# Values of all heads multiplied first as token rows, input with features on partitions

## The chip, the cores and the metric

The kernel runs on one core of one Trainium2 chip. The time is what the device takes for one execution, in microseconds (us). The core has a matrix engine (TensorE, PE in the profile), a vector engine (VectorE, DVE), a scalar engine (ScalarE, ACT), a general engine (GpSimd, POOL) and a queue engine (SyncE, SP) that issues transfers. SBUF is the memory of 128 partitions from which the engines read; PSUM holds the results of PE in 8 banks of 128 x 512 floats.

## What is computed

An encoder layer over two sequences, 512 and 1024 tokens of 1024 features, processed as 1536 token rows. The part that matters here is the mixer:

```python
def hybrid_mixer(h, w_in, w_fnet, lb_f, lb_b, out_norm, w_out):
    proj = h @ w_in                       # h = rms_norm(x, norm_mix)
    u, q, zf, zb, iv, g = jnp.split(proj, cuts, axis=-1)
    ...                                   # u: Fourier mixing, 4 groups of 128
    qh = jax.nn.silu(q)                   # 4 heads of 128
    vh = iv.reshape(bsz, seq, HGRN_HEADS, HGRN_DV)
    k_f, logf_f = hgrn2_gates(zf, lb_f)
    k_b, logf_b = hgrn2_gates(zb, lb_b)
    o_fwd = chunked_gated_recurrence(qh, k_f, vh, logf_f)
    o_bwd = ...                           # the same backwards, with k_b, logf_b
    gate = jax.nn.silu(g)
    y_rec = rms_norm(o_fwd + o_bwd, out_norm) * gate
    return jnp.concatenate([y_fourier, y_rec], axis=-1) @ w_out
```

rms_norm(x) is x * rsqrt(mean(x * x) + eps) * w, per token. Behind the mixer come a router and 16 experts, each of which takes its best tokens.

## The kernel before

A product of 32-bit numbers is made of three matmuls of numbers split in a high and a low part (`three_products`, L62 to L66). `heads_phase` (L255) is the first stage; the transform, the router and the experts follow in code of their own.

**The start.** `InputNorm` (L153) loads the 12 input tiles of 128 token rows, takes the sum of squares with ACT (L195), scales rows on DVE (L224), turns each tile on PE with 8 transposes (L249), copies the high part on ACT (L213) and subtracts the low part on DVE (L237). The features of the normalized input (`big_hi`, `big_lo`) then lie on partitions. From the fourth tile on, PE's turns are interleaved with products V, G and Q of the first block (`EARLY`). `HeadWeights` (L69) loads the projection weights in halves of 128x512 (L88), rounds them on ACT (L92) and subtracts on POOL (L96).

**Projections.** 4 heads x 3 blocks of 512 tokens give NN = 12 rounds n. A head has five: values V, gate G, queries Q and the two forget gates ZF and ZB; 12 more belong to the Fourier groups. Each takes 24 matmuls of 512 columns in two halves, `begin` and `proj`, into one of two banks (`PJ`). V comes out with features on partitions, and event `vt` turns it into token rows (L827, copied by ACT at L578 into `v_tok`).

**Rounds.** A list `timeline` gives one order for all engines. Round n has 8 slots. Slot s holds `level` s: 32 small matmuls (L853) that need ACT's copy of keys (L526), which in turn needs DVE's scaling of keys and queries (L720, L722). Then follow the recurrence steps (`update` on DVE, `inter` on PE), the DVE gates of a projection that ended one slot before (`take_gates`), and halves of coming projections, `FILL` of them: 1, 1, 1, 1, 1, 2, 2, 1. Rounds with n % 3 = 0 carry the recurrence of blocks 1 and 2, those with n % 3 = 1 that of block 0; they end with `square`, `ss` (sum of squares, root on ACT at L626), `rstd`, `bc` (a broadcast by PE, L905) and `out` (the product on DVE, L768). Behind slot 7 come `intra` (L864) and `kt`, the turn of the keys (L872). `out` frees the bank into which `kt` goes. The gates of ZB are the longest on DVE: L695, L697, L699, L700, L701. The last matmuls of the stage are L912. The order itself:

## Time and profile before

| | us |
|---|---|
| median of three executions | 2577.06 |
| lowest and highest | 2575.56, 2579.19 |
| the profiled execution | 2577.25 |
| its span, first to last instruction | 2575.5 |
| PE busy in it | 2520.0 |
| DVE busy, ACT busy | 1649.2, 1366.9 |
| heads stage, from the start to the end of L912 | 568.4 |

The span has three stretches: the heads stage, the transform and router up to about 800 us, and the experts. Round 0 begins (its level 0) at 66.47 us. A row of a timeline gives start and duration in us, the engine, line, operation and its tiles; in brackets the idle time before it and what ended it. A row of `--lines` kind gives a group: busy time, mean ns of one, idle time.

### The profile page before, as it was taken

What the parts mean: (1) busy time and instruction counts of PE and PEld (TensorE: products, weight loads), DVE (VectorE), ACT (ScalarE), POOL (GpSimd) and SP (SyncE); (2) the same over time, 40 slices, a digit from 0 to 9 for tenths busy, and PEclk for the clock granted to TensorE, in tenths of its full rate; (3) what the DMA queues carried; (4) which work ended last, traced back from release to release, by engine and by line L of the source; (5) the groups of instructions that cost most, each with busy time, mean ns of one, the idle gap of its engine ahead of it and who ended that gap; (6) DMA issues with size and microseconds to landing.
All of it is one profiled execution on the core that took longest, in us unless ns stands there. A gap on an engine that the chain in (4) does not pass through costs nothing.

```text
span 2575.5 us, 45337 instructions
## 1 busy us (share of the span) xinstructions
PE 2520.0 (98%) x18610; PEld 2278.5 (88%) x18610; DVE 1649.2 (64%) x1927; ACT 1366.9 (53%) x1559; POOL 266.7 (10%) x238
## 2 busy tenths in 40 slices
PE   8999999999987999999999999999999999999998
PEld 6777777787876999999999999999999999999997
DVE  6555555435387666767666676666767666676667
ACT  6434353424445555555556555555555556555556
POOL 3102020101101010010101101010010101101010
PEclk9999999999997999999999999999999999999999
DMA  4101010135327676676767667676676767667677
GB/s 158 31 17 55 2 55 2 61 122 209 138 96 298 229 253 234 247 252 228 252 228 252 240 241 252 228 252 233 247 252 228 252 228 252 240 241 252 228 253 282
DMA packets 62486, 503.73 MB, mean 196 GB/s; under 512 B 7568, under 2 KB 8080, under 8 KB 37808
## 3 DMA queue, kind: packets, MB, share of 16 engines
q1 hardware_dynamic: 46224, 448.88, 48.0%
q0 software_dynamic: 16160, 53.38, 7.0%
q8 instruction: 77, 1.26, 0.2%
q14 instruction: 25, 0.20, 0.0%
HBM read 465.07 MB, written 37.22 MB: 195 GB/s over the span
## 4 chain that ended last, share of the span: by engine, by line
PE 67%; DVE 1%; ACT 1%; DMA 0%; issue 0%; POOL 0%; POOLq 0%; DVEq 0%; ACTq 0%
PE up_banks_b L2025 15%; PE up_banks_a L2025 15%; PE up_banks_b L2028 6%; PE up_banks_a L2028 6%; PE up_banks_b L2061 2%; PE up_banks_b L2060 2%; PE up_banks_b L2059 2%; PE up_banks_b L2058 2%; PE up_banks_a L2062 2%; PE up_banks_b L2062 2%; PE up_banks_a L2059 2%; PE up_banks_a L2061 2%; PE up_banks_a L2058 2%; PE up_banks_a L2060 2%; PE up_banks_b L2023 1%; PE up_banks_a L2023 1%
## 5 line engine op out<-in xcount | busy, mean ns | idle before, releaser
L1842 DVE TENSOR_TENSOR big_lo<-ew_raw,big_hi 128x4096 fp32r<-128x4096 f32 x192 | 849.6, 4425 | 419.0 <-ACT big_hi L1653 418.9
L1653 ACT CAST big_hi<-ew_raw 128x4096 fp32r<-128x4096 f32 x192 | 697.3, 3632 | 506.5 <-PE up_banks_a L2025 223.7
L2025 PE MATMUL up_banks_b<-x_parts,big_hi 128*128 128x384 f32 x2048 | 582.9, 356 | 0.0
L2025 PE MATMUL up_banks_a<-x_parts,big_hi 128*128 128x384 f32 x2016 | 573.8, 356 | 0.0
L2028 PE MATMUL up_banks_b<-x_parts,big_lo 128*128 128x192 f32 x1792 | 449.0, 251 | 0.0
L2028 PE MATMUL up_banks_a<-x_parts,big_lo 128*128 128x192 f32 x1764 | 442.0, 251 | 0.0
L2025 PEld LDWEIGHTS up_banks_b<-x_parts,big_hi 128*128 128x128 f32 x2048 | 371.0, 189 | 0.0
L2025 PEld LDWEIGHTS up_banks_a<-x_parts,big_hi 128*128 128x128 f32 x2016 | 365.1, 189 | 0.6
L2028 PEld LDWEIGHTS up_banks_b<-x_parts,big_lo 128*128 128x128 f32 x1792 | 341.4, 191 | 0.0
L2028 PEld LDWEIGHTS up_banks_a<-x_parts,big_lo 128*128 128x128 f32 x1764 | 336.1, 191 | 0.6
L64 PE MATMUL bank<-big_hi,w_hi 128*128 128x512 f32 x576 | 236.8, 411 | 0.0
L66 PE MATMUL bank<-big_hi,w_lo 128*128 128x512 f32 x576 | 225.6, 392 | 0.0
L65 PE MATMUL bank<-big_lo,w_hi 128*128 128x512 f32 x576 | 225.3, 391 | 0.0
L1639 POOL DMA_INDIRECT residual<-table,this_token x15 | 24.2, 1613 | 1426.5 <-DVE yp L1956 1426.5
L720 DVE TENSOR_TENSOR kq<-kq,decay 128x512 f32<-128x512 f32 x84 | 58.0, 691 | 175.5 <-PE bank L853 175.5
L66 PEld LDWEIGHTS bank<-big_hi,w_lo 128*128 128x128 f32 x576 | 108.4, 188 | 24.1
L64 PEld LDWEIGHTS bank<-big_hi,w_hi 128*128 128x128 f32 x576 | 108.5, 188 | 22.5
L65 PEld LDWEIGHTS bank<-big_lo,w_hi 128*128 128x128 f32 x576 | 108.7, 189 | 19.2
L526 ACT COPY keys<-kq 128x512 f32<-128x512 f32 x84 | 55.6, 662 | 113.1 <-DVE kq L722 112.5
L96 POOL TENSOR_TENSOR w_lo<-w_raw,w_hi 128x512 fp32r<-128x512 f32 x48 | 72.1, 1515 | 406.8 <-ACT w_hi L92 406.7
L1674 ACT CAST h_parts<-ups 128x384 fp32r<-128x384 f32 x128 | 65.5, 511 | 78.4 <-DVE ups L1908 78.4
L2062 PE MATMUL up_banks_a<-big_lo,h_parts 128*128 128x512 f32 x256 | 99.6, 389 | 0.0
(320 smaller groups left out, 4076.3 us busy)
## 6 DMA issues: line engine op xcount, KB each, us to landing
ew_raw<-in_expert_weights SPq DMA_DIRECT2D x192, 2048.0 KB, 7.8
w_raw<-in_w_heads SPq DMA_DIRECT2D x48, 256.0 KB, 2.8
x_in<-in_x SPq DMA_DIRECT2D x12, 512.0 KB, 4.4
x_d<-in_x POOLq DMA_DIRECT2D x12, 512.0 KB, 4.1
residual<-x_d POOLq DMA_DIRECT2D x12, 512.0 KB, 2.9
ffn_in<-h_and_xT_d POOLq DMA_DIRECT2D x12, 512.0 KB, 2.9
ew_raw<-residual SPq DMA_DIRECT2D x12, 512.0 KB, 6.7
tab<-in_tables POOLq DMA_DIRECT2D x10, 512.0 KB, 7.6
```

Of the source, the lines that this page charges most:

```text
L64: nc.tensor.matmul(out, w_hi, x_hi, start=start, stop=False, skip_group_check=True)
L65: nc.tensor.matmul(out, w_hi, x_lo, start=False, stop=False, skip_group_check=True)
L66: return nc.tensor.matmul(out, w_lo, x_hi, start=False, stop=stop, skip_group_check=True)
L1653: nc.scalar.copy(w_hi[:, c % RING], raw[:, c % RAW]).then_inc(hi_done, 1)
L1842: nc.vector.tensor_tensor(w_lo[:, c % RING], raw[:, c % RAW], w_hi[:, c % RING].bitcast(F32), ALU.subtract).then_inc(lo_done, 1)
L2025: last = nc.tensor.matmul(out[:, 0:2 * CAP], hi, x[:, k], start=n == 0, stop=n == KT - 1, skip_group_check=True)
L2028: nc.tensor.matmul(out[:, ALL_HI], lo, x[:, k, ALL_HI], start=False, stop=False, skip_group_check=True)
L2058: nc.tensor.matmul(s_bank[i], h[:, t, S_HI], hi, start=a, stop=False)
L2059: nc.tensor.matmul(s_bank[i], h[:, t, H_S_LO], hi, start=False, stop=False)
L2060: nc.tensor.matmul(s_bank[i], h[:, t, S_HI], lo, start=False, stop=b)
L2061: nc.tensor.matmul(p_bank[i], h[:, t, H_P_BOTH], hi, start=a, stop=False)
L2062: last = nc.tensor.matmul(p_bank[i], h[:, t, H_P_BOTH], lo, start=False, stop=b)
```

## The change

The host also hands over the input with features on partitions (`x_cols`) and the norm weights as columns. The 96 turns of the input, the 48 turns of the values and their copies disappear. Instead:

- `InputNorm` keeps x as 8 tiles of 128x512 per block. Squares are made on ACT (L234) and added on DVE (L243) into one accumulator; PE sums them over the partitions with a column of ones (`total`, L251, 4 matmuls of one column per block), ACT takes the root, DVE inverts, PE spreads the result over the partitions (`spread`, L272), and DVE multiplies (L279), ACT copies (L295), DVE subtracts (L299).
- Values are made first, for all four heads at once: a stationary tile of 128 tokens, 512 columns of weights (L947 to L949), 12 token tiles of 24 matmuls. The first four tiles use block 0 before it is normalized (only the norm weight is in it, L284, L289); the rows are scaled by ACT when they leave PSUM (L665). Block 0 is normalized last.
- Values are stored to DRAM (L539) and loaded into `v_tok` by head and block (L552).
- Value weights come in four pieces of 128x1024. DVE subtracts the first two, POOL the others (L100).
- The sums and spreads stand at fixed places in PE's products (`lines`).
- The stream of projections has G, Q, ZF and ZB; `FILL` is one half in every slot; in rounds with n % 3 = 0 the gate of the round after next is projected between Q and ZF.

```diff
 LEVELS = 7
 EPS = 1e-6
-HEAD_SRC = (4, 5, 1, 2, 3)
+HEAD_SRC, VALUE_SRC = (5, 1, 2, 3), 4
 NJ = len(HEAD_SRC)
...
+    PIECES = ((0, 1), (2, 3), (4, 5, 6, 7))
+    LINES = [("sum", 0), ("sum", 1), ("spread", 1), ("sum", 2), ("spread", 2), ("spread", 0)]
+    SCALED = ([("rstd", 0), ("rstd", 1)] + [(1, k) for k in range(KT)] + [("rstd", 2)] +
+              [(b, k) for b in (2, 0) for k in range(KT)])
+    SPLIT = [(b, k) for b in ("raw", 1, 2, 0) for k in range(KT)]
...
+    def add(self, dve, b, k):
+        n = KT * b + k
+        dve.wait_ge(self.squared, n + 2)
+        if k > 1:
+            dve.wait_ge(self.added, self.adds(n - 1))
+        elif b:
+            dve.wait_ge(self.totalled, self.LINES.index(("sum", b - 1)) + 1)
+        self.nc.vector.tensor_tensor(self.added_up, self.squares[0] if k == 1 else self.added_up, self.squares[n % 2], ALU.add)\
+            .then_inc(self.added, 1)
...
+    def total(self, pe, b):
+        pe.wait_ge(self.added, (KT - 1) * (b + 1))
+        if b == 2:
+            pe.wait_ge(self.scaled, self.SCALED.index((1, KT - 1)) + 1)
+        for c in range(CH):
+            last = self.nc.tensor.matmul(self.totals[b][:, c:c + 1], self.added_up[:, c * P:(c + 1) * P], self.ones[:],
+                                         start=c == 0, stop=c == CH - 1, skip_group_check=True)
+        last.then_inc(self.totalled, 1)
+
...
+        VALUE_TILES = [(tuple(range(CH)), bank[0:CH])] + \
+                      [((t, t + 1), pair) for t, pair in ((4, o_acc[1:3]), (6, bank[0:2]), (8, bank[2:4]), (10, o_acc[1:3]))]
+        VALUES_OUT = 16 * TT // 2
+        V_FIRST = [16 * NB * len(ks) for ks in norm.PIECES]
...
-            stream += proj(n, V) + [("begin", n, G), ("vt", n), ("proj", n, G)]
-            stream += [e for j in (Q, ZF, ZB) for e in proj(n, j)]
+            ahead = {1: ((n, G), (n, Q), (n + 1, G), (n, ZF), (n, ZB)), 2: ((n, Q), (n, ZF), (n, ZB))}
+            stream += [e for m, j in ahead.get(n % NB, ((n, G), (n, Q), (n, ZF), (n, ZB))) for e in proj(m, j)]
...
-        FILL, LAST_FILL = (1, 1, 1, 1, 1, 2, 2, 1), (2, 2, 2, 1, 1, 1, 1, 1)
+        FILL, LAST_FILL = (1,) * 8, (2, 2, 2, 1, 1, 1, 1, 1)
...
+                for t in range(TT):
+                    sp.wait_ge(v_evicted, t + 1)
+                    sp.dma_start(v_dram[t * P:(t + 1) * P], sig[:, t % 2]).then_inc(sig_used[t % 2], 16)
+
+                def load_values(n):
+
+                    h, b = n // NB, n % NB
+                    if h == 0:
+                        for i in range(2):
+                            sp.wait_ge(sig_used[i], VALUES_OUT)
+                        norm.parted(sp, 1, KT - 1)
+                    else:
+                        filled(sp, ("u", n - NB, 0))
+                        filled(sp, ("u", n - NB, 1))
+                        sp.wait_ge(intra_done, n - NB + 1)
+                    sp.dma_start(v_tok[:, b], v_dram[b * BLK:(b + 1) * BLK, h * P:(h + 1) * P]
+                                 .rearrange("(c p) v -> p c v", p=P)).then_inc(norm.loaded[b], 16)
+
...
+                def evict_values(tiles):
+
+                    for t in tiles:
+                        act.wait_ge(v_filled, 1 + next(i for i, (ts, _) in enumerate(VALUE_TILES) if t in ts))
+                        if t >= 2:
+                            act.wait_ge(sig_used[t % 2], 16 * (t // 2))
+                        value = next(flat(banks[ts.index(t)][:]) for ts, banks in VALUE_TILES if t in ts)
+                        if t < CH:
+                            norm.inverted(act, 0)
+                            nc.scalar.activation(sig[:, t % 2], value, ACT.Identity, scale=norm.rstd[:, t:t + 1])\
+                                .then_inc(v_evicted, 1)
+                        else:
+                            nc.scalar.copy(sig[:, t % 2], value).then_inc(v_evicted, 1)
+
...
+                act.wait_ge(const_loaded, 64)
+                norm.high_raw(act, 0)
+                norm.high_raw(act, 1)
+                weights.high_values(act, 0)
+                norm.high_raw(act, 2)
+                norm.high_raw(act, 3)
+                weights.high_values(act, 1)
+                squares(0, 0, 1, 2, 3)
+                for k in range(4, KT):
+                    norm.high_raw(act, k)
+                squares(0, 4, 5, 6, 7)
+                weights.high_values(act, 2)
+                weights.high_values(act, 3)
+                squares(1, *range(KT))
+                weights.high(act, 0)
+                weights.high(act, 1)
+                norm.root(act, 0)
+                norm.root(act, 1)
+                for k in range(KT):
+                    norm.high(act, 1, k)
+                evict_values(range(0, 4))
+                squares(2, *range(KT))
+                norm.root(act, 2)
+                evict_values((4, 5))
+                for k in range(KT):
+                    norm.high(act, 2, k)
+                evict_values((6, 7))
+                for k in range(KT):
+                    norm.high(act, 0, k)
+                evict_values((8, 9))
+                evict_values((10, 11))
+                for m in (2, 3):
+                    weights.high(act, m)
                 for ev in timeline:
...
+                dve.wait_ge(const_loaded, 64)
+                norm.low_raw(dve, 0)
+                norm.low_raw(dve, 1)
+                weights.low_values(dve, nc.vector, 0)
+                norm.low_raw(dve, 2)
+                norm.low_raw(dve, 3)
+                weights.low_values(dve, nc.vector, 1)
+                for k in range(1, 4):
+                    norm.add(dve, 0, k)
+                for k in range(4, KT):
+                    norm.low_raw(dve, k)
+                for k in range(4, KT):
+                    norm.add(dve, 0, k)
+                add_squares(1)
+                norm.invert(dve, 0)
+                norm.invert(dve, 1)
+                normalize_block(1)
+                add_squares(2)
+                norm.invert(dve, 2)
+                normalize_block(2)
+                dve.wait_ge(v_filled, 1)
+                normalize_block(0)
                 dve.wait_ge(mask_loaded, 16)
...
+                lines = {(0, 4): ("sum", 0), (0, 5): ("sum", 1), (0, 6): ("spread", 1),
+                         (6, 1): ("sum", 2), (6, 3): ("spread", 2), (8, 3): ("spread", 0)}
+                for tiles, banks in VALUE_TILES:
+                    t = tiles[0]
+                    if t in free_after:
+                        pe.wait_ge(v_evicted, free_after[t])
+                    for k in range(KT):
+                        if t == 0 and k % 2 == 0:
+                            pe.wait_ge(weights.lo_done, k // 2 + 1)
+                        norm.parted(pe, "raw" if t < CH else t // CH, k)
+                        last = values(k, tiles, banks)
+                        if (t, k) in lines:
+                            line, b = lines[t, k]
+                            (norm.total if line == "sum" else norm.spread)(pe, b)
+                    last.then_inc(v_filled, 1)
+                pe.wait_ge(v_evicted, 10)
+                norm.parted(pe, 0, KT - 1)
```

PE near the start of the program. In the kernel before, the first instructions are turns of the rows:

```order
L249 MATMUL o_acc<-ident_a,h_rows 128x128 [waits h_ready,const_loaded_a]
L249 MATMUL o_acc<-ident_a,h_rows 128x128 x7
L249 MATMUL o_acc<-ident_a,h_rows 128x128 [waits h_ready]
L249 MATMUL o_acc<-ident_a,h_rows 128x128 x3
L249 MATMUL bank<-ident_a,h_rows 128x128 x4
```

In the changed kernel this is PE in tiles 6 and 7 (the third pair of banks), from the second k step on:

```order
L947 MATMUL bank<-w_hi,big_hi 128x512
L948 MATMUL bank<-w_hi,big_lo 128x512
L949 MATMUL bank<-w_lo,big_hi 128x512
L251 MATMUL o_acc<-ones,state 128x1 [waits x_scaled,x_squares_added]
L251 MATMUL o_acc<-ones,state 128x1 x3
L947 MATMUL bank<-w_hi,big_hi 128x512 [waits h_lo_done]
L948 MATMUL bank<-w_hi,big_lo 128x512
```

Where the turns stood behind DVE's rows, PE now stands at a sum (L251) behind the additions (`x_squares_added`) and the normalized block 1 (`x_scaled`). This is ACT of the changed kernel ahead of the third root, in the same stretch:

```order
L295 CAST big_hi<-kq 128x512 [waits x_scaled] x4
L295 CAST big_hi<-v_tok 128x512 [waits x_scaled] x3
L295 CAST big_hi<-scores 128x512 [waits x_scaled]
L665 ACTIVATE sig<-bank,x_rstd 128x512 [waits x_scaled,v_filled] x2
L665 ACTIVATE sig<-bank,x_rstd 128x512 [waits x_scaled,sig_used0,v_filled]
L665 ACTIVATE sig<-bank,x_rstd 128x512 [waits x_scaled,sig_used1,v_filled]
L234 ACTIVATE k_tok<-kq 128x512 [waits x_squares_added,in_loaded0] x2
L234 ACTIVATE k_tok<-kq 128x512 [waits x_squares_added,in_loaded1] x2
L234 ACTIVATE k_tok<-gate 128x512 [waits x_squares_added,in_loaded2] x4
L257 ACTIVATE x_rms<-o_acc,eps_b 128x4 [waits x_totalled]
```

The four evictions of values (L665) have moved in front of the squares of block 2 (L234), and two of them wait for a store (`sig_used`). The third place is DVE from level 6 to the end of round 3. Before:

```order
L695 TENSOR_SCALAR kq1<-sig,one_less_lb 128x512 [waits sig_ready]
L697 TENSOR_SCALAR decay0<-kq1 128x512 [waits dve_step]
L699 TENSOR_TENSOR k_sum<-kq1 128x512 [waits dve_step]
L700 TENSOR_TENSOR kq1<-q,decay0 128x512
L701 TENSOR_TENSOR kq1<-q,decay0 128x512 [waits dve_step]
L717 TENSOR_TENSOR chunk_decay<-decay6 128x8 [waits kq_up]
L720 TENSOR_TENSOR kq0<-kq0,decay6 128x8x64 [waits bank_filled2]
L722 TENSOR_TENSOR kq0<-kq0,decay6 128x8x64
L731 COPY scores<-bank2 64x4x64 [waits intra_done]
L759 RECIPROCAL o_rstd<-o_rms 128x8 [waits bank_read4]
L768 TENSOR_TENSOR gate<-gate,bank4 128x512 [waits bank_filled4,o_weighed]
L768 TENSOR_TENSOR gate<-gate,bank3 128x512 [waits bank_filled3,o_weighed]
```

And in the changed kernel:

```order
L886 TENSOR_TENSOR chunk_decay<-decay6 128x8 [waits kq_up]
L889 TENSOR_TENSOR kq0<-kq0,decay6 128x8x64 [waits bank_filled3]
L891 TENSOR_TENSOR kq0<-kq0,decay6 128x8x64
L900 COPY scores<-bank3 64x4x64 [waits intra_done]
L928 RECIPROCAL o_rstd<-o_rms 128x8 [waits bank_read4]
L864 TENSOR_SCALAR kq1<-sig,one_less_lb 128x512 [waits sig_ready]
L866 TENSOR_SCALAR decay0<-kq1 128x512 [waits dve_step]
L868 TENSOR_TENSOR k_sum<-kq1 128x512 [waits dve_step]
L869 TENSOR_TENSOR kq1<-q,decay0 128x512
L870 TENSOR_TENSOR kq1<-q,decay0 128x512 [waits dve_step]
L937 TENSOR_TENSOR gate<-gate,bank4 128x512 [waits bank_filled4,o_weighed]
L937 TENSOR_TENSOR gate<-gate,bank2 128x512 [waits bank_filled2,o_weighed]
```

The gates of ZB (L695 to L701, now L864 to L870) have moved from behind level 6 to between the reciprocal of the root and the two output products (L768, now L937). On ACT of the changed kernel the same stretch reads:

```order
L733 COPY scores<-near 32x4x32 [waits bank_read3,intra_done]
L733 COPY scores<-near 32x4x32 x3
L736 COPY scores<-bank 32x4x32 x4
L764 ACT_TABLE_LOAD
L764 ACTIVATE o_rms<-bank,eps_b 128x8 [waits bank_filled4]
L648 ACT_TABLE_LOAD [waits bank_filled0]
L648 ACTIVATE sig<-bank 128x512 [waits sig_used0]
L741 COPY scores<-bank 64x4x64 [waits sig_ready,bank_filled3]
```

The sigmoid of ZB (L648) with its table load now stands behind the root (L764); before, it stood ahead of the copies of scores.

## Rows read from the trace of the kernel before

**Rows 1.** The page: busy time of each engine, share of the span, instructions.

```profile
PE 2520.0 (98%) x18610; PEld 2278.5 (88%) x18610; DVE 1649.2 (64%) x1927; ACT 1366.9 (53%) x1559; POOL 266.7 (10%) x238
```

**Rows 2.** Timeline of PE: start, duration, operation, idle time before it.

```profile
8.44 1.94 PE L249 MATMUL o_acc<-ident_a,h_rows 128*128 128x128 f32 x8 [8.44 <-DVE h_rows L224]
...
19.66 1.97 PE L249 MATMUL o_acc<-ident_a,h_rows 128*128 128x128 f32 x8 [0.89 <-DVE h_rows L224]
...
23.13 0.63 PE L65 MATMUL bank<-big_lo,w_hi 128*128 128x512 f32 x1
...
25.55 0.40 PE L64 MATMUL bank<-big_hi,w_hi 128*128 128x512 f32 x1
...
46.43 0.60 PE L827 MATMUL bank<-ident_b,sig 128*128 128x128 f32 x4
```

**Rows 3.** Timeline of PE, 45 products apart.

```profile
52.34 0.39 PE L64 MATMUL bank<-big_hi,w_hi 128*128 128x512 f32 x1
...
62.54 0.39 PE L64 MATMUL bank<-big_hi,w_hi 128*128 128x512 f32 x1
```

**Rows 4.** Waits of PE up to 600 us: total, times, longest.

```profile
PE o_acc L249 <- DVE h_rows L224: 12.7, 6, 8.4
PE bank L905 <- ACT v_tok L578: 2.5, 3, 0.8
...
PE bank L853 <- ACT keys L526: 0.9, 3, 0.3
```

**Rows 5.** Stretches: PE, PEld, DVE, ACT, POOL busy, granted clock, DMA share, GB/s.

```profile
2.00:8.00 6.00, 0.00 (x0) 0.00 (x0) 1.15 (x2) 1.68 (x5) 0.15 (x2) 1.00 0.97 316
8.00:14.00 6.00, 3.93 (x17) 3.16 (x17) 4.47 (x8) 5.15 (x11) 0.00 (x0) 1.00 1.00 352
33.00:36.00 3.00, 3.00 (x20) 2.57 (x19) 2.50 (x4) 2.14 (x5) 1.29 (x1) 1.00 0.89 279
...
770.00:775.00 5.00, 2.23 (x72) 1.70 (x72) 4.18 (x13) 4.46 (x7) 0.53 (x1) 0.65 0.26 105
```

**Rows 6.** Groups from 0 to 80 us, and from the whole page (last row).

```profile
L96 POOL TENSOR_TENSOR w_lo<-w_raw,w_hi 128x512 fp32r<-128x512 f32 x10 | 18.7, 1873 | 24.0 <-ACT w_hi L92 24.0
...
L224 DVE SCALAR_TENSOR_TENSOR h_rows<-x_in,x_rstd,norm_mix_rows 128x1024 f32<-128x1024 f32 x12 | 15.4, 1285 | 0.4
...
L92 ACT CAST w_hi<-w_raw 128x512 fp32r<-128x512 f32 x10 | 6.1, 610 | 2.0 <-DMA w_raw<-in_w_heads 2.0
...
L96 POOL TENSOR_TENSOR w_lo<-w_raw,w_hi 128x512 fp32r<-128x512 f32 x48 | 72.1, 1515 | 406.8 <-ACT w_hi L92 406.7
```

**Rows 7.** The page: DMA issues, KB each, us to landing.

```profile
w_raw<-in_w_heads SPq DMA_DIRECT2D x48, 256.0 KB, 2.8
```

**Rows 8.** Timeline: round 0's level 0, and the stage's last matmuls.

```profile
66.47 0.32 PE L853 MATMUL bank<-q,k_sum 128*32 128x32 f32 x14
...
566.48 1.95 PE L912 MATMUL o_acc<-fourier_space 128*128 128x128 f32 x16
```

**Rows 9.** Timeline of a quiet round (11): key copy, and the level it feeds.

```profile
503.30 0.62 ACT L526 COPY keys<-kq 128x512 f32<-128x512 f32 x1 [2.67 <-DVE kq L722]
...
504.77 0.32 PE L853 MATMUL bank<-kq,keys 128*32 128x32 f32 x14
```

**Rows 10.** Timeline of a heavy round (3), DVE, ACT and the next level 0.

```profile
204.43 0.69 DVE L720 TENSOR_TENSOR kq<-kq,decay 128x512 f32<-128x512 f32 x1 [1.43 <-PE bank L853]
...
205.65 0.48 DVE L695 TENSOR_SCALAR kq<-sig,one_less_lb 128x512 f32<-128x512 f32 x1
...
208.67 0.16 DVE L717 TENSOR_TENSOR chunk_decay<-decay 128x8 f32<-128x8 f32 x1
...
208.60 1.28 ACT L626 ACT_TABLE_LOAD   x1
...
209.89 0.27 ACT L626 ACTIVATE o_rms<-bank,eps_b 128x8 f32<-128x8 f32 x1
...
218.95 0.24 PE L853 MATMUL bank<-q,k_sum 128*32 128x32 f32 x4
```

371 lines of the change are left out of this document (191 added, 180 removed).

## The prediction

> **What bounds the kernel now.** I read the page's busy shares first: TensorE (PE) is busy for 98% of the span [rows 1]. So a change counts only by what it does to PE's stream: work taken out, clock lost, waits opened. The change touches the heads stage, from the start to the products that build the Fourier matrices at 568.4 us [rows 8]; everything behind it is the same code. I therefore balance PE's time up to that point. The timeline of the start comes next: PE first runs at 8.44 us, and a 512-column matmul at 23.13 us takes 0.63 us, at 25.55 us 0.40 us [rows 2]: first the 1.2 GHz level, then the 2.4 GHz level, though the granted-clock column prints 1.00 for both. From 52.34 to 62.54 us 45 of them take 10.20 us, 0.227 us each [rows 3], the 2.4 GHz level. When the transposed value block starts at 46.43 us, PE has done 72 products (16.3 us at that rate): 30.1 us of the start is not product. The waits of PE say what is lost to others: 12.7 us for the normalized rows at the start, then 2.5 and 0.9 us in the rounds [rows 4], 3.4 us.
>
> The other view is one slot of a quiet round. The level at 504.77 us follows one half projection; the key copy that it needs runs from 503.30 for 0.62 us [rows 9]. So a slot with one half has 0.85 us to spare. This is the spare that the change spends: before, slots 5 and 6 of a round had two halves.
>
> **Part 1, what leaves.** The product count stays: 288 value products (12 x 24) move to the front, same shape. Half a projection is 12 x 0.227 = 2.72 us. The 96 input transposes and the row normalization go with the whole old start. In the rounds each value transposition costs 0.44 us on PE (an estimate: four of them show 0.60 us [rows 2], and some 0.16 us of that lies under the next matmul), and the 3.4 us of waits can go. From the first level 0 (66.47) to 568.4 us before takes 502.0 us [rows 8]. It holds 20 value halves, and the changed order is 2 other halves further at that point: 22 x 2.72 = 59.8. Less 10 x 0.44 = 4.4 and 3.4: **434.4 us** of rounds if no new wait opens.
>
> **Part 2, the new start.** PE, ACT and DVE all wait for the four small constants, though the first block is there before. The three last of these are queued behind block 0 (2.10 MB) and two value pieces (1.05 MB). The queue moved 316 GB/s from 2 to 8 us [rows 5]; 3.15 MB from 2.6 us, plus 0.6 to land, is 13.2 us (12.1 to 14.5 for the 352 and 279 GB/s of two later stretches). I take 316, because it is the rate of the same moment. Then two scaled copies and a 1024-wide cast on ACT (2 x 0.6 + 0.9; a 512-wide cast is 0.61 [rows 6]) and the 1024-wide subtraction on DVE (1.2; the 128x1024 DVE row is 1.28 [rows 6]): PE starts at **16.6 us**, 8 us later than now, but straight on products. 288 x 0.227 = **65.4**. The old start's last dense stretch began at 19.66 us and was slow at least until 23.13 [rows 2]; 3.8 us at half speed cost **1.8**. Three sums of 4 and three spreads of 4 matrices add **3.3** (0.2 and 0.9; a spread is like a broadcast of the rounds).
>
> Waits inside it. (a) Weight pieces 2 and 3 are subtracted on POOL. A 512-wide one takes 1.87 us in the busy start and 1.4 after it ((72.1 - 18.7) / 38) [rows 6]. DVE is mostly idle when these pieces run, so I take 2.7 for 1024. ACT has its cast done at 26.8 (from 15.3: a cast, eight squares and six copies of 0.6 us that wait for DVE's additions twice). Piece 2 is ready at 29.5, PE at 29.3: **0.2** (up to 1.3 with 3.8 us a piece). (b) The second sum stands on PE one k step (2.7 us) behind the first. But the first addition of block 1 waits for the first sum, since both use one accumulator, and ACT's squares hang on it by their two buffers: seven additions of 0.6 us, half of them behind a square, are a chain of 5.3 us. PE waits **2.6**. (c) The third sum stands after two k steps of tiles 6 and 7. Its squares stand on ACT behind eight copies of block 1 and four value evictions, and the third eviction waits for the first one's store (2.2 us). From the spread of block 1 (41.7 us) that gives 51.6 for the copies, 55.7 for the evictions, 62.3 for the additions; PE is there at 58.3: **4.0**. Where PE was busy for 2.2 of 5 us, from 770 us on, the granted clock fell (mean 0.65 [rows 5]), that is to the 1.2 GHz level in part; I book half of such a fall, **0.9**. The value stage ends at 16.6 + 65.4 + 1.8 + 3.3 + 0.2 + 2.6 + 4.0 + 0.9 = **94.8 us**.
>
> The Trainium skill (GPSIMD Engine Reference, section Specifications) says that GpSimd's SBUF interfaces are shared with VectorE when that has two SBUF inputs. The trace agrees: POOL's subtraction averages 1.87 us beside the busy DVE of the start [rows 6]. By it piece 2 would take 3.8 us and (a) would cost 1.3 us.
>
> Then four projections (21.8 us), three halves (8.2), and one wait: the weights of ZF are loaded only after the last value store has landed and three value loads are issued, near 6 us after the stage's end. 2.8 us to landing [rows 7], cast and subtraction of two halves make 13.1 us, PE wants them at 10.9: **2.2**. The first level 0 comes at 94.8 + 32.2 = **127.0 us**.
>
> **Part 3, the rounds with one half per slot.** Three kinds of round. Heavy ones (n = 3, 6, 9) carry the recurrence of two blocks, and here the gates of ZB move from slot 6 into slot 7. In before's clock: DVE had waited 1.43 us for level 6 [rows 10], which now comes early, so ACT's root table and root, done at 210.16, are done at 208.8. Only then comes the sigmoid's table and ZB's sigmoid (1.28 + 0.60: 210.7), which stood before them until now; then ZB's gates, 3.02 us from 205.65 to 208.67 [rows 10]: 213.7. The output product that frees PE's bank for the key turn is queued on DVE behind these gates: 214.4, level 0 at 215.3. Without waits it would be 218.95 - 5.44 (two halves) - 0.44 - 0.84 = 212.2: **3.1 us** each, 9.3 in all. Rounds 1, 4, 7, 10: ZB's gates (3.0 us) and the output product now stand on DVE ahead of level 6, and the table loads delay level 5's keys: **1.0** each, 4.0. Rounds 2, 5, 8: the gates end 5.0 us into slot 5, keys 7.1 us, PE comes at 6.7: **0.5** each, 1.5. Rounds 0 and 11: 0. Sum **14.8 us** (4 to 22: below, ACT and DVE keep the order but the output product is early; above, every round behaves like a heavy one by half).
>
> The skill (ScalarE: Activation LUTs, What ACT_TABLE_LOAD costs) gives a switch of tables 2.66 us with a drain. Here the load takes 1.28 and the root starts 0.01 us behind it [rows 10], so the measurement decides. By the page the heavy rounds would lose up to 2.8 us more each.
>
> **The sum.** 127.0 + 434.4 + 14.8 = 576.2 us against 568.4: **+7.8 us**. The profiled execution took 2577.25 us (span 2575.5), 0.2 above the median. Forecast: **2585.0 us**, slower by 0.3%. The gain in the rounds is real, but the stage in front has the same overhead as the old start (94.8 - 65.4 = 29.4 against 30.1), and the slots' spare is spent.
>
> **Rivals.**
> - A: the slots' spare holds. If DVE reaches the output product and the gates as soon as PE needs them (most spare slots show 0.85 us [rows 9], DVE is only 64% busy [rows 1]), the rounds lose 3 us instead of 14.8, and the start loses 3 less: 2585.0 - 14.8 = **2570 us**. It speaks against it that in heavy rounds the order itself puts the gates ahead. It decides if the added waits in the rounds stay under 5 us. Chance 0.24.
> - B: half of both waits: **2577 us**, no change. For it speaks that each term was worked out with mean durations that overlap by up to 0.1 us. Chance 0.16.
> - C: the constants land at 14.5 us, POOL takes 3.8 us a piece, the clock falls at each of the two waits, and the rounds lose 18: 2585.0 + 1.3 + 1.1 + 2.5 + 3.2 = **2593 us**. Chance 0.14.
> - D: the ends of the change differ but the start begins at once: the first products don't wait for block 0's rest if the small transfers overtake it. They are in the same queue, and the second input tile, queued behind others, landed in turn. It would give 2580 and lies within the forecast's case.
>
> **Numbers.** Forecast's case 0.46 (2580 to 2590). 0.2% is about 5 us, which is what a measurement of this kernel can tell from no change. Slower than 2582.3: 0.38 of the forecast's case and all of C, 0.52. Same: 0.08 of the forecast, 0.13 of B, 0.03 of A: 0.24. Faster: 0.21 of A, 0.03 of B: 0.24. Range 2567 to 2597: it takes in A at 2570 and C with 4 us for the unseen rate of 1 KB rows.
>
> **What would show it.** First product near 16.6 us, and DVE's and ACT's first work at 13.2. PE's waits at the sums: near 0, 2.6 and 4 us, released by DVE's additions. Level 0 of round 0 at 127 us. In rounds 3, 6 and 9 PE's key turn waits about 3 us for DVE's output product; PE's waits for keys in the other rounds stay under 1 us each. The first product of the transform stage comes near 577 us. If waits in the rounds are under 5 us, part 3 was wrong; if level 0 comes before 120 us, part 2 was. A matmul that streams the weights of four heads (four pieces of 128 columns) slower than 0.227 us would break part 1.

## The result and the profile after

The changed kernel takes **2616.66 us** (median of four, 2613.21 to 2617.60) against 2576.59 us for the kernel before, run beside it: the ratio is 1.0152, with a 95% interval of 1.0134 to 1.0169. That is 40 us slower where 8 were forecast; the range ended at 2597. The profiled execution has a span of 2615.8 us. The heads stage ends at 605.19 + 1.95 = 607.1 us instead of 568.4 [rows 8], 38.7 later; behind it 2008.7 us follow instead of 2007.1. So the loss is where the forecast looked for it.

The page of the changed kernel, busy time of each engine, answers to [rows 1]:

```profile
PE 2525.6 (97%) x18514; PEld 2280.2 (87%) x18514; DVE 1681.4 (64%) x1960; ACT 1366.0 (52%) x1542; POOL 251.6 (10%) x232
```

DVE has 32 us more busy time. Where most of POOL's subtraction work is left out (below), DVE's busy time falls by 22.7 us in this kernel (to 1658.7), and by 11.9 in the kernel before (to 1637.3): so much of DVE's busy time is operations that take longer beside POOL.

Waits of PE up to 620 us (total, times, longest), the view of [rows 4]:

```profile
PE bank L947 <- DVE w_lo L100: 18.2, 1, 18.2
PE bank L1017 <- ACT keys L626: 15.0, 11, 2.6
PE o_acc L251 <- DVE state L243: 8.2, 2, 4.7
PE bank L1036 <- DVE gate L937: 6.7, 3, 2.2
PE bank L64 <- POOL w_lo L125: 1.6, 1, 1.6
...
PE bank L1069 <- DVE o_rstd L928: 1.0, 3, 0.3
```

Timeline of PE: first product, the second and third sum, ZF's first half, level 0 of round 0, the end of the stage:

```profile
18.21 0.76 PE L947 MATMUL bank<-w_hi,big_hi 128*128 128x512 f32 x1 [18.21 <-DVE w_lo L100]
...
41.70 1.87 PE L251 MATMUL o_acc<-ones,state 128*128 128x1 f32 x8 [3.44 <-DVE state L243]
...
70.25 1.87 PE L251 MATMUL o_acc<-ones,state 128*128 128x1 f32 x8 [4.75 <-DVE state L243]
...
119.38 0.47 PE L64 MATMUL bank<-big_hi,w_hi 128*128 128x512 f32 x1 [1.61 <-POOL w_lo L125]
...
138.64 0.46 PE L1017 MATMUL bank<-q,k_sum 128*32 128x32 f32 x32
...
605.19 1.95 PE L1076 MATMUL o_acc<-fourier_space 128*128 128x128 f32 x16
```

Level 0 of round 0 was forecast for 127.0 us and comes at 138.6, 11.6 late; the rounds from there to the end of the stage were to take 449.2 us (434.4 + 14.8) and take 468.5, 19.3 more. Together these are the 30.9 us between 38.7 and the forecast 7.8.

Where the rounds lose it, the table shows: us from one level 0 to the next, for two of the kernels below too.

| rounds | before | changed | POOL's work left out | other halves per slot |
|---|---|---|---|---|
| 0 | 34.5 | 28.5 | 28.5 | 29.5 |
| 1, 4, 7, 10 | 39.1, 38.9, 38.9, 38.4 | 36.6, 39.0, 39.0, 39.0 | 33.8, 35.1, 35.4, 33.8 | 33.6, 34.5, 33.6, 34.7 |
| 2, 5, 8 | 36.4 each | 30.7, 30.8, 30.8 | 30.7 each | 30.3, 30.3, 30.2 |
| 3, 6, 9 | 42.6 each | 39.5, 39.6, 39.6 | 39.1, 38.9, 38.9 | 38.3, 37.7, 38.1 |
| 11, to the stage's end | 75.4 | 75.5 | 75.4 | 75.4 |

Two half projections (5.44 us) and a transposition of values (0.44) have left each of the rounds 0 to 10. Rounds 0, 2, 5 and 8 are shorter by that, within 0.3 us. Rounds 3, 6 and 9 give half of it back, as forecast. Rounds 1, 4, 7 and 10 give back nearly all, four of them together 153.5 us where 134.9 were forecast: this is the miss. Round 4 of the changed kernel, DVE, ACT, POOL and PE in slots 5 to 7 (a key copy made in slot 5 feeds PE's level 6, one made in slot 6 feeds PE's level 7, the last):

```profile
297.85 0.60 ACT L648 ACTIVATE sig<-bank 128x512 f32<-128x512 f32 x1
...
298.56 1.14 ACT L121 CAST w_hi<-w_raw 128x512 fp32r<-128x512 f32 x2
...
299.25 3.12 POOL L125 TENSOR_TENSOR w_lo<-w_raw,w_hi 128x512 fp32r<-128x512 f32 x2 [7.28 <-ACT w_hi L121]
299.58 1.64 DVE L868 TENSOR_TENSOR k_sum<-kq 128x512 f32<-128x512 f32 x1
299.60 0.61 ACT L626 COPY keys<-kq 128x512 f32<-128x512 f32 x1
300.36 0.46 PE L1017 MATMUL bank<-kq,keys 128*32 128x32 f32 x32 [0.89 <-ACT keys L626]
301.14 1.78 DVE L869 TENSOR_TENSOR kq<-q,decay 128x512 f32<-128x512 f32 x1
...
305.56 0.62 ACT L626 COPY keys<-kq 128x512 f32<-128x512 f32 x1 [5.35 <-DVE kq L891]
...
306.32 0.69 PE L1017 MATMUL bank<-kq,keys 128*32 128x64 f32 x32 [2.56 <-ACT keys L626]
```

The reader is to see two operations of ZB's gates at 1.64 and 1.78 us, which elsewhere take 0.69 each, and POOL's two subtractions of weights over just that time: 2.05 us, in a chain (sigmoid, gates, output product, scaling, key copy) at whose end PE waits 2.56 us. Ahead of it, ACT's two casts of those weights hold back the key copy of slot 5: 0.89 us. And behind such waits the clock can fall. Columns as in [rows 5]; first round 1, then round 4, around PE's level 7:

```profile
197.00:202.00 5.00, 3.42 (x44) 2.89 (x45) 3.36 (x7) 3.58 (x11) 0.00 (x0) 1.00 0.02 3
```

```profile
305.00:310.00 5.00, 3.68 (x39) 2.99 (x40) 3.14 (x7) 3.58 (x11) 0.00 (x0) 0.68 0.00 0
```

With the same waits (0.92 and 2.56; 0.89 and 2.56) the granted clock stays up in round 1 (1.00) and falls in round 4 (mean 0.68), which is 2.4 us longer. Its products behind the wait follow each other in 0.43 us, those of round 1 in 0.23.

### The profile page after: what moved, and what is told of

The parts are those of the page before. It is cut to its first block, busy times and chain, and to the rows that moved or that the text cites. A ratio compares the mean times of both kernels' runs of the same rounds, so it can differ in the third digit from the quotient of the medians.

```text
span 2615.8 us, 45189 instructions
## 1 busy us (share of the span) xinstructions
PE 2525.6 (97%) x18514; PEld 2280.2 (87%) x18514; DVE 1681.4 (64%) x1960; ACT 1366.0 (52%) x1542; POOL 251.6 (10%) x232
## 4 chain that ended last, share of the span: by engine, by line
PE 66%; DVE 1%; ACT 1%; issue 0%; POOL 0%; DVEq 0%; POOLq 0%; ACTq 0%
PE up_banks_b L2189 15%; PE up_banks_a L2189 15%; PE up_banks_a L2192 6%; PE up_banks_b L2192 6%; PE up_banks_b L2225 2%; PE up_banks_b L2223 2%; PE up_banks_b L2224 2%; PE up_banks_b L2222 2%; PE up_banks_a L2226 2%; PE up_banks_b L2226 2%; PE up_banks_a L2225 2%; PE up_banks_a L2223 2%; PE up_banks_a L2222 2%; PE up_banks_a L2224 2%; PE up_banks_b L2187 1%; PE up_banks_a L2187 1%
## 5 line engine op out<-in xcount | busy, mean ns | idle before, releaser
L64 PE MATMUL bank<-big_hi,w_hi 128*128 128x512 f32 x480 | 200.5, 418 | 1.6 <-POOL w_lo L125 1.6
L66 PE MATMUL bank<-big_hi,w_lo 128*128 128x512 f32 x480 | 189.2, 394 | 0.0
L65 PE MATMUL bank<-big_lo,w_hi 128*128 128x512 f32 x480 | 188.8, 393 | 0.0
L64 PEld LDWEIGHTS bank<-big_hi,w_hi 128*128 128x128 f32 x480 | 91.3, 190 | 21.3 <-issue 2.3
L66 PEld LDWEIGHTS bank<-big_hi,w_lo 128*128 128x128 f32 x480 | 91.0, 190 | 20.7
L65 PEld LDWEIGHTS bank<-big_lo,w_hi 128*128 128x128 f32 x480 | 91.7, 191 | 16.0
L2223 PE MATMUL up_banks_a<-big_hi,h_parts 128*128 128x512 f32 x256 | 99.6, 389 | 0.0
```

The source lines that it names most:

```text
L64: nc.tensor.matmul(out, w_hi, x_hi, start=start, stop=False, skip_group_check=True)
L65: nc.tensor.matmul(out, w_hi, x_lo, start=False, stop=False, skip_group_check=True)
L66: return nc.tensor.matmul(out, w_lo, x_hi, start=False, stop=stop, skip_group_check=True)
L2223: nc.tensor.matmul(s_bank[i], h[:, t, H_S_LO], hi, start=False, stop=False)
```

## The experiments

Line numbers of the kernels made for this are up to 9 higher than in the changed kernel. All are edits of the changed kernel, but the one that starts from the kernel before.

**Without POOL's work in the rounds.** The question: does POOL's subtraction lengthen DVE's gates, or is it the order alone?

```diff
-        self.nc.gpsimd.tensor_tensor(self.half(self.lo, m), self.raw[:, m % 2], self.half(self.hi, m).bitcast(F32),
-                                     ALU.subtract).then_inc(self.lo_done, 1)
+        lo, raw, hi = (x[:, :, 0:8] for x in (self.half(self.lo, m), self.raw[:, m % 2], self.half(self.hi, m)))
+        self.nc.gpsimd.tensor_tensor(lo, raw, hi.bitcast(F32), ALU.subtract).then_inc(self.lo_done, 1)
...
+                nc.gpsimd.memset(w_lo[:, 0].bitcast(F32), 0.0)
```

> The changed kernel, with one thing left out: GpSimd's subtraction of a half of projection weights (L125) covers 8 of each 128 columns only, 48 instructions of some 0.2 us in place of 1.4 us; the low parts of the other columns are left as they were, so the sums are not the reference's. Nothing else moves. Theory P (two engines disturb each other): in rounds 1, 4, 7 and 10 two gate operations of DVE took 1.64 and 1.78 us beside the subtraction instead of 0.69; without it the wait of PE at level 6 falls from 2.56 to some 0.5 us, the 0.9 us at level 5 stays (it is ACT's two casts), four rounds give back 8 us and, where the clock then stays up, up to 6 more: 2602 to 2609 us. Theory O (the order alone): the gates and the output product ahead of level 6 cost the wait whatever POOL does; it stays at 2.3 to 2.6 us and the time within 2 us of 2616.7.

Measured: 2597.6 us, 19.0 below the changed kernel (ratio to the kernel before 1.0076, 1.0060 to 1.0093). Groups of DVE from 160 to 600 us (busy time, mean ns), first of the changed kernel, then of this one:

```profile
L869 DVE TENSOR_TENSOR kq<-q,decay 128x512 f32<-128x512 f32 x11 | 11.9, 1082 | 0.0
L868 DVE TENSOR_TENSOR k_sum<-kq 128x512 f32<-128x512 f32 x11 | 11.4, 1037 | 0.4
```

```profile
L870 DVE TENSOR_TENSOR kq<-q,decay 128x512 f32<-128x512 f32 x11 | 7.8, 705 | 0.0
L869 DVE TENSOR_TENSOR k_sum<-kq 128x512 f32<-128x512 f32 x11 | 7.6, 693 | 0.4
```

The two groups lose 3.8 and 4.1 us, some 2 us for each of the four rounds, and the same place of round 4 reads:

```profile
293.42 0.50 PE L1018 MATMUL bank<-kq,keys 128*32 128x32 f32 x32 [0.60 <-ACT keys L627]
297.39 0.65 PE L1018 MATMUL bank<-kq,keys 128*32 128x64 f32 x32 [0.51 <-ACT keys L627]
```

Theory P holds, and the order alone (theory O) is out: 2.56 became 0.51. The gain is larger than expected. The rounds 1, 4, 7 and 10 give 15.5 us, of which the waits are 9.2 (four times 3.45 less 1.15) and the other 6.3 the clock; 1.8 come from rounds 3, 6 and 9, and ZF's first wait is 0.5 instead of 1.61 us. Another 2.2 us ahead of level 0 of round 0, from an earlier start and the clock, are within what such executions differ by (last section).

**POOL left out of the kernel before.** If the disturbance is there too, does it cost anything?

```diff
-        self.nc.gpsimd.tensor_tensor(self.half(self.lo, m), self.raw[:, m % 2], self.half(self.hi, m).bitcast(F32),
-                                     ALU.subtract).then_inc(self.lo_done, 1)
+        count = P if m < 2 * NJ else 8
+        lo, raw, hi = (x[:, :, 0:count] for x in (self.half(self.lo, m), self.raw[:, m % 2], self.half(self.hi, m)))
+        self.nc.gpsimd.tensor_tensor(lo, raw, hi.bitcast(F32), ALU.subtract).then_inc(self.lo_done, 1)
```

> The kernel before, with GpSimd's subtraction of weights cut to 8 of 128 columns from head 1 on (38 of its 48 instructions; the sums are then not the reference's). In it DVE's operations are stretched in the same slot (1.79 and 1.51 us instead of 0.69 at 247.5 and 249.3 us), but two halves of projection stand in slots 5 and 6. Theory P with spare: PE doesn't wait there, so nothing is won: within 2 us of 2576.7. If the same disturbance cost PE time in the kernel before too, it would be 5 to 15 us faster and the difference between the kernels would not be explained by it.

Measured: 2576.4 us, ratio 1.0002 (0.9993 to 1.0011). The kernel before has stretched operations too, at about the same place of round 4, but they are others: the second scaling of slot 6 and the first of ZB's gates.

```profile
247.42 3.06 POOL L96 TENSOR_TENSOR w_lo<-w_raw,w_hi 128x512 fp32r<-128x512 f32 x2 [2.10 <-ACT w_hi L92]
247.54 1.79 DVE L722 TENSOR_TENSOR kq<-kq,decay 128x512 f32<-128x512 f32 x1
...
249.26 1.51 DVE L695 TENSOR_SCALAR kq<-sig,one_less_lb 128x512 f32<-128x512 f32 x1
```

There it costs nothing. So the change did not bring the disturbance, it made it cost time. It did two things to these rounds at once: it took one of the two halves out of slot 5 and out of slot 6, and it moved ZB's gates from behind the scaling of slot 6 to ahead of it. No run here separates the two.

**The half of slot 0 in slot 5.**

```diff
-        FILL, LAST_FILL = (1,) * 8, (2, 2, 2, 1, 1, 1, 1, 1)
+        FILL, LAST_FILL = (0, 1, 1, 1, 1, 2, 1, 1), (2, 2, 2, 1, 1, 1, 1, 1)
```

> The changed kernel, with half projections per slot of 0, 1, 1, 1, 1, 2, 1, 1 instead of one each: the half of slot 0, where PE also has the update products, stands in slot 5. Theory S (spare at one place): in rounds 1, 4, 7 and 10 slot 5 then offers PE 2.7 us more of work while DVE makes the gates, the waits of 0.9 and 2.6 us and the clock lost behind them go, and slot 0 costs under 1 us per round: 2598 to 2606 us. Rival M (moved wait): slot 0 without a half makes PE wait for the keys of level 1 in all 11 rounds by 1 to 2 us and nothing is won: 2612 to 2625 us.

Measured: 2593.8 us, 22.9 below the changed kernel. Waits of PE up to 610 us:

```profile
PE bank L1036 <- DVE gate L937: 5.7, 3, 1.9
PE bank L1017 <- ACT keys L626: 2.7, 5, 1.1
PE bank L64 <- POOL w_lo L125: 2.2, 1, 2.2
PE o_acc L1028 <- DVE scores L900: 1.7, 4, 0.4
```

Keys cost 2.7 us in five waits instead of 15.0 in eleven. Slot 0 without a half costs 1.0 us in round 0 alone: in the others the update products fill it. The gain is above the expectation. Rounds 1, 4, 7 and 10 get back 17.0 of the 18.6 us that they lose beyond the forecast, with the same number of products.

But it is not theory S as it was written, a second half beside the gates. The half that left slot 0 also ends ZB's projection one slot later, and its gates with it. Round 4:

```profile
294.98 0.69 DVE L937 TENSOR_TENSOR gate<-gate,bank 128x512 f32<-128x512 f32 x1 [4.18 <-PE bank L1069]
295.59 1.01 DVE L886 TENSOR_TENSOR decay<-decay 128x16 f32<-128x16 f32 x1
...
297.73 0.47 DVE L864 TENSOR_SCALAR kq<-sig,one_less_lb 128x512 f32<-128x512 f32 x1
...
298.60 0.65 PE L1017 MATMUL bank<-kq,keys 128*32 128x64 f32 x32 [0.38 <-ACT keys L626]
```

DVE waits 4.18 us in slot 5 for PE's broadcast, then makes the output product and the scaling, and only then (297.73) the gates of ZB, undisturbed. The gates have left the chain ahead of PE's level 7, as in the kernel before, and the casts stand behind the key copy of slot 5. POOL's subtraction now falls on a 128x16 operation (1.01 us) and costs PE 0.38 us at most. How much of the gain is the order, and how much the second half in slot 5, this run does not say.

**The casts later.** Can the disturbance be moved away instead?

```diff
+                held = None
...
                         if n % NB == NB - 1:
-                            split_weights(n // NB + 1, j)
+                            if j == ZB and n < NN - 1:
+                                held = [n // NB + 1, 2]
+                            else:
+                                split_weights(n // NB + 1, j)
...
+                        if held:
+                            held[1] -= 1
+                            if held[1] == 0:
+                                split_weights(held[0], ZB)
+                                held = None
```

> The changed kernel; ACT's two casts of the weights that stand behind ZB's projection (and with them POOL's two subtractions) are made two key copies later, behind the copies of scores of level 6, in rounds 1, 4 and 7. Nothing is left out. Theory P (POOL's subtraction stretches DVE's gates by 2.05 us, the casts delay level 5's keys by 0.9): both waits fall to 0.5 us and 0 in rounds 1, 4 and 7, as where POOL's work was left out, and the clock stays up in 4 and 7; three rounds of four give back 3 to 5.5 us each: 2602 to 2607 us. Rival L (the disturbance only moves): POOL's two operations now run beside level 7's scaling and the gates of the next slot, and DVE is late there: 2610 to 2617 us.

Measured: 2608.9 us, 7.7 below the changed kernel, between the two expectations. Round 4:

```profile
295.99 0.69 DVE L877 TENSOR_TENSOR k_sum<-kq 128x512 f32<-128x512 f32 x1
296.60 0.68 DVE L878 TENSOR_TENSOR kq<-q,decay 128x512 f32<-128x512 f32 x1
...
300.69 0.65 PE L1026 MATMUL bank<-kq,keys 128*32 128x64 f32 x32 [1.48 <-ACT keys L626]
...
304.84 1.16 PE L1037 MATMUL o_acc<-scores,v_tok 128*128 128x128 f32 x8 [0.55 <-ACT scores L750]
```

The gates are undisturbed and the wait of 0.89 us is gone; 1.48 us remain, and 0.55 new ones arise where the casts now stand ahead of a copy of scores. Rounds 1, 4 and 7 take 35.3, 36.2 and 35.4 us, round 10, in which nothing was moved, 39.1. So of the 3.45 us that PE waits in such a round, 1.1 to 1.5 belong to the order (1.1 to 1.2 are left without POOL's work, 1.5 here), which was forecast at 1.0, and 2.0 to 2.3 to POOL.

**The output products ahead of ZB's gates in rounds 3, 6 and 9.**

```diff
-                timeline += at_slot[s] + take_gates()
+                gates = take_gates()
+                behind = s == 7 and n % NB == 0
+                timeline += at_slot[s] + ([] if behind else gates)
                 timeline += take_halves(FILL[s] if n < NN else LAST_FILL[s]) + at_end[s]
+                timeline += gates if behind else []
```

> The changed kernel; in rounds with n % 3 = 0 the gates that stand in slot 7 (ZB's) come behind the two output products instead of ahead of them. Theory H (the forecast's mechanism for the heavy rounds): PE's wait of 2.24 us at the key turn of rounds 3, 6 and 9 is the time of the gates; it goes, level 0 of the next round then waits up to 0.5 us for the key sum; 1.8 us plus the lost clock (0.8 us) a round: 2608 to 2612 us. Rival K (moved wait): DVE idles until PE's broadcast is there and the later gates delay level 0 and the keys of level 1 by the same 2 us: 2615 to 2618 us.

Measured: 2606.8 us, 9.9 below. The wait of 2.24 us at the key turn is gone, and level 0 waits in its place:

```profile
270.12 0.46 PE L1020 MATMUL bank<-q,k_sum 128*32 128x32 f32 x32 [0.79 <-DVE k_sum L871]
```

Rounds 3, 6 and 9 take 37.3 us each instead of 39.5. This makes 6.8 us; most of the rest is not the edit's doing: PE starts 0.8 us earlier in this execution, and the clock lost 2.4 us less in the value stage (below), where the code is the same.

**The sums of the value stage moved.**

```diff
-                evict_values(range(0, 4))
+                evict_values((0, 1))
                 squares(2, *range(KT))
                 norm.root(act, 2)
+                evict_values((2, 3))
                 evict_values((4, 5))
...
-                lines = {(0, 4): ("sum", 0), (0, 5): ("sum", 1), (0, 6): ("spread", 1),
-                         (6, 1): ("sum", 2), (6, 3): ("spread", 2), (8, 3): ("spread", 0)}
+                lines = {(0, 2): ("sum", 0), (0, 5): ("sum", 1), (0, 6): ("spread", 1),
+                         (6, 3): ("sum", 2), (6, 4): ("spread", 2), (8, 3): ("spread", 0)}
```

> The changed kernel, with three moves in the value stage: the first sum of squares stands behind the third k step of the first four tiles instead of the fifth; ACT squares block 2 between the second and third value eviction instead of behind the fourth; the third sum and its spread stand behind k steps 4 and 5 of tiles 6 and 7 instead of 2 and 4. Theory W: the two waits of PE (3.4 and 4.75 us) came from the chain of additions that starts with the first sum and from the evictions; both go, and with them 21 products at the 1.2 GHz level (0.43 instead of 0.227 us each, 4.3 us), the slower sums 2 us: 14 us, 2602 to 2604 us. Rival N: DVE's and ACT's work is what fills the stage; the waits return at tiles 4 or 8, where the normalized rows of blocks 1 and 2 are needed, and the gain is under 5 us.

Measured: 2604.2 us, 12.5 below. Timeline of PE, the three sums:

```profile
27.88 1.05 PE L251 MATMUL bank<-ones,state 128*128 128x1 f32 x8 [0.74 <-DVE state L243]
...
37.83 1.05 PE L251 MATMUL o_acc<-ones,state 128*128 128x1 f32 x8 [0.59 <-DVE state L243]
...
61.55 0.95 PE L251 MATMUL o_acc<-ones,state 128*128 128x1 f32 x8
```

Waits of 8.2 us have become 1.3 (and one new of 0.7 for a low part), and a sum takes 0.95 to 1.05 us where it took 1.87 behind a wait: the clock no longer falls there. Theory W holds.

**The constants first.** The same three lines are taken out behind block 0.

```diff
                 sp.dma_start(norm.nm[:], norm_mix_cols).then_inc(const_loaded, 16)
+                sp.dma_start(ident[:], identity).then_inc(const_loaded, 16)
+                sp.dma_start(onorm[:], out_norm).then_inc(const_loaded, 16)
+                sp.dma_start(lb[:], lb_params).then_inc(const_loaded, 16)
```

> The changed kernel, with the loads of identity, output norm and bounds (three small ones) issued right behind the norm weights, ahead of block 0. Theory Q (queueing decides): they landed at 14.4 us, although the first two input tiles and the first value piece were there before. Now ACT begins when the first tile has landed (4 to 6 us), PE at 9 to 11 us instead of 18.2, and the whole program ends 7 to 9 us earlier: 2608 to 2610 us. Rival B (bytes decide): tiles and value pieces are 4.2 MB at 350 GB/s, so a start before 12 us only opens waits between the first k steps and the gain is under 4 us.

Measured: 2611.4 us, 5.3 below: more than rival B allows and less than theory Q wants. PE starts at 11.93 instead of 18.21 us, so queueing did decide; but ACT's first work began at 7.14 us, when the first tile had landed (issued at 2.62), not at 4 to 6, and the cast of the first value piece at 9.36. The landing of the first transfers was taken too short.

**All four together.** The diffs are those above.

> The changed kernel with four edits together: constants first, the sums of the value stage moved, halves per slot 0, 1, 1, 1, 1, 2, 1, 1, and the output products ahead of ZB's gates in rounds with n % 3 = 0. If the edits add up (5.3 + 12.5 + 22.9 us measured alone, and 6 us for the last): 2567 to 2572 us, 0.2 to 0.4% faster than the kernel before. If the earlier start meets the sums (block 2's tiles are loaded only when the value pieces are subtracted, and the chain of additions starts earlier), 3 to 5 us of it are lost: 2572 to 2577 us.

Measured: 2571.4 us, ratio to the kernel before 0.9976 (0.9966 to 0.9986): faster than both kernels, than the one before by 0.24%. The four single gains sum to 50.6 us; together they give 45.3.

**One half per slot and the later casts, with the other three edits.**

> The same as the kernel with all four edits, but one half in every slot and the later casts behind ZB's projection instead of the other halves per slot. With the waits of rounds 1, 4 and 7 gone by the later casts alone, round 10 unchanged: 2572 to 2580 us. It is slower than the four edits together if slot 5 of round 10 and the waits of 0.4 us of level 7 remain.

Measured: 2581.9 us (1.0019, 1.0010 to 1.0029), 1.9 above the range expected. The halves per slot do more than the later casts: rounds 1, 4, 7 and 10 take 35.3, 35.4, 35.4 and 36.6 us here and 33.6 to 33.9 with all four edits.

**A semaphore for the norm weights alone.** It takes the place of the edit that put the constants first: the three other constants are back behind block 0, and PE awaits them at the first sum only. The other three edits stay.

```diff
-                sp.dma_start(norm.nm[:], norm_mix_cols).then_inc(const_loaded, 16)
+                sp.dma_start(norm.nm[:], norm_mix_cols).then_inc(norm.nm_loaded, 16)
...
-                act.wait_ge(const_loaded, 64)
+                act.wait_ge(norm.nm_loaded, 16)
...
-                dve.wait_ge(const_loaded, 64)
+                dve.wait_ge(norm.nm_loaded, 16)
...
+                dve.wait_ge(const_loaded, 48)
...
-                pe.wait_ge(const_loaded, 64)
...
+                            if (line, b) == ("sum", 0):
+                                pe.wait_ge(const_loaded, 48)
```

> The four edits together (2571.4 us), but the three small constants stay behind block 0 and the norm weights get a semaphore of their own: ACT and DVE begin on these alone, the other constants are awaited at the first sum. The first tile is then issued at 1.2 us instead of 2.6. If the issue sets the start: PE starts at 10.6 instead of 12.05 us, 2569.5 to 2570.5 us. If PE then only waits longer at the first sum or for piece 2, nothing is won: 2571 to 2572 us.

Measured: **2569.0 us**, ratio 0.9969 (0.9957 to 0.9981), 7.1 us below the kernel before. PE starts at 9.57 us instead of 12.05 with all four edits, but level 0 of round 0 comes at 120.04 instead of 120.96, only 0.9 us earlier: ZF's first half waits 2.16 us for its weights instead of 1.78, and behind that wait the granted clock is 0.57 (99 to 103 us), where with all four edits it was 1.00 (101 to 105 us).

**Value pieces 2 and 3 on DVE.** The last kernel, with POOL's two 1024-wide subtractions made by DVE.

> The same, and value pieces 2 and 3 are subtracted by DVE (1.23 us each) instead of GpSimd (5.17 us for both, while DVE's seven additions beside it took 7.1 us instead of 5.3). Theory P (the two disturb each other): DVE loses 2.5 us and gets 1.8 back, piece 2 is ready earlier; PE's waits at the sums and at tile 4 (2.3 us together) stay within 1 us: equal within 1.5 us, 2568 to 2571.5 us. If the waits at sum 1 and tile 4 grow by DVE's added 2.5 us, then 2572 to 2574 us.

Measured: 2569.0 us, 0.9971 (0.9960 to 0.9983). Equal, as theory P has it: six additions of squares beside the pieces take 4.67 us instead of 6.03, and DVE spends 2.36 us on the pieces.

## Why the prediction was wrong

The direction was right and the places too; two terms were mis-sized, one of them because a cost was left out.

- **Part 1.** 288 products took 0.227 us each once the clock was up. The floor of the rounds holds: rounds 0, 2, 5 and 8 are within 0.3 us of before less 5.88 (5.44 + 0.44). Right.
- **The start.** Forecast 16.6 us, measured 18.2. The constants landed at 14.4 where 13.2 was taken, close to the upper bound given (14.5). Right in kind. (The terms given for the start add up to 16.5, not 16.6.)
- **The sums.** Forecast waits 2.6 and 4.0 us, measured 3.44 and 4.75: the mechanism was right. **The clock behind them was booked at 0.9 us,** half of one fall; it fell at both. Nine products behind the second sum and twelve behind the third followed each other in 0.43 instead of 0.227 us, 4.3 more; two sums and a spread took 1.7, 1.7 and 1.2 us instead of 0.8, 2.2 more. That is 6.5 us, a step short by 5.6. A sum takes as long as a spread, 0.8 us, not 0.2: with 0.1 on the product behind each, the six cost 5.5 at full clock instead of 3.3. The slow start cost 2.6 (twelve products) instead of 1.8, and the two waits, with the tail of the product ahead of each, took 8.5 instead of 6.6. The stage ended at 106.7 instead of 94.8: 1.6 from the start, 5.6, 2.2, 0.8 and 1.9 from these terms.
- **To level 0.** 31.9 us behind the value stage, forecast 32.2; the wait for ZF's weights 1.6, forecast 2.2. Right.
- **Rounds 3, 6, 9.** Forecast 3.1 us each, measured 0.32 + 2.24 of waits and about 1.1 of clock: 3.7. Showing the output products first removed the wait. Right.
- **Rounds 2, 5, 8.** Forecast 0.5 each, measured 0.3 to 0.4. Right.
- **Rounds 1, 4, 7, 10: the step that failed.** "1.0 each, 4.0" was 3.7 in round 1 and 6.2 to 6.5 in the others, some 22.6. The step took ZB's gates at 3.0 us, as in an undisturbed slot, and the table loads as the other cost. It left out that ACT's casts and POOL's subtraction of the same projection's weights come in that very slot. What the order costs was near the forecast (1.1 to 1.5 against 1.0). The disturbance adds 2.0 to 2.3 us of wait, and the whole wait costs, three times in four, 2.4 us of clock more than the fourth time.

The prediction did use the rule on the shared SBUF interfaces: the Trainium skill (GPSIMD Engine Reference, section Specifications) gives contention with VectorE instructions that have two SBUF inputs or run in a 2-port perf mode. But it weighed only what POOL loses by it, at the start. The runs show the other side: k_sum and the product of queries, both with two SBUF inputs, took 1.64 and 1.78 us for 0.69. The like of these rows stood in the trace of the kernel before (1.79 us at 247.54), where no wait hung on it. An operation with one such input was stretched there as well (L695: 1.51 for 0.48 us); in which mode it ran no trace shows.

Rival A (the slots' spare holds) was wrong for the same reason; rival C named late constants, the clock and more loss in the rounds, all of which came, but with 18 us of loss in the rounds where 34 came about. The upper bound of the unknown costs was set by "every round like a heavy one", and the heavy rounds were not the worst.

## What to carry to other kernels

Before work is taken out beside an engine that waits for nothing, look for operations that run longer than their like there: they may be costs which the work covers. A slot is to be priced with the durations that it has under its neighbours' load, and with all that ACT and POOL do in it, not with the mean. Where the filler is fixed in number, ask also what its place does to the order: one number moved in a table (slot 0 to slot 5) was worth 23 us, and with it the gates left the chain on which PE waited. A wait of PE is to be priced with the clock behind it: here the same waits cost 2.4 us more of slow matmuls in three rounds of four than in the fourth.

## What the runs showed of the hardware

- The VectorE operations that were stretched here began while GpSimd subtracted, and ended a fixed time after the subtraction did. They look held until its end, not slowed. Changed kernel, the subtractions one by one (the DVE rows beside the first two, 299.58 and 301.14, stand above):

```profile
299.25 1.42 POOL L125 TENSOR_TENSOR w_lo<-w_raw,w_hi 128x512 fp32r<-128x512 f32 x1 [7.28 <-ACT w_hi L121]
300.63 1.74 POOL L125 TENSOR_TENSOR w_lo<-w_raw,w_hi 128x512 fp32r<-128x512 f32 x1
...
174.86 1.28 POOL L125 TENSOR_TENSOR w_lo<-w_raw,w_hi 128x512 fp32r<-128x512 f32 x1
174.90 1.32 DVE L910 COPY state<-kq 128x128 f32<-128x128 f32 x1
...
150.08 1.64 POOL L125 TENSOR_TENSOR w_lo<-w_raw,w_hi 128x512 fp32r<-128x512 f32 x1 [25.91 <-ACT w_hi L121]
150.68 0.68 DVE L846 TENSOR_TENSOR gate<-sig,bank 128x512 f32<-128x512 f32 x1
```

  The subtractions end at 300.67 and 302.37 us, the two DVE operations at 301.22 and 302.92, each 0.55 later; so it is in all eight cases of rounds 1, 4, 7 and 10. A copy of 128x128, whose like takes 0.24 us in the mean with POOL's work left out, takes 1.32 and ends 0.08 us after the subtraction. An operation that reads its second input from PSUM (`bank`, L846) is not touched: 0.68 us. So what such an operation loses is about what is left of the subtraction, and a small one loses as much as a large one: the 128x16 one of the kernel with other halves took 1.01 us too.
- What a wait costs in clock depends on when it falls. Round 1 and round 4 of the changed kernel have the same waits, within 0.03 us, and differ by 2.4 us. Round 1 itself took 36.6 us in the changed kernel and with the constants first, 38.2 where only the sums or only the output products of rounds 3, 6 and 9 were moved; its code is the same in all four. From the first product to level 0 of round 0 it took 120.4 us in the changed kernel and 118.0 in the two with later casts and with the output products first, whose code up to there is the same; from 44 to 48 us the granted clock was 0.58 in the first and 0.74 in the last, of which a part is that PE started 0.8 us earlier there. The sum behind the same wait of 3.44 us, which took 1.87 us in the changed kernel, shows it without that: 1.05 us with the output products first (the row below the two).

```profile
44.00:48.00 4.00, 4.00 (x12) 3.15 (x11) 0.08 (x1) 0.00 (x0) 0.00 (x0) 0.58 0.44 125
```

```profile
44.00:48.00 4.00, 4.00 (x19) 3.36 (x18) 0.67 (x2) 0.00 (x0) 0.00 (x0) 0.74 0.24 69
```

```profile
40.90 1.05 PE L251 MATMUL o_acc<-ones,state 128*128 128x1 f32 x8 [3.44 <-DVE state L243]
```

So a difference of 2 to 3 us between two such kernels may be this alone. What sets it is open. It also enters the 5.3 us by which the four edits together fall short of the sum of their single gains: the heads stages of the profiled executions are shorter by 53 us one by one and by 45 together, and 6.3 of the missing 8 lie ahead of level 0 of round 0, where the kernel with the output products first had gained 3.3 by an earlier start and a milder fall of the clock, which the other edits remove anyhow. The rest is open.
